# First weights, convolution steps, prompt set-up and sample loads moved to earlier stages of a two-layer hybrid decoder step

## The chip, the core and the metric

The kernel runs on one core of a Trainium2 chip. A core has TensorE (PE, matrix products into PSUM), VectorE (DVE), ScalarE (ACT), GpSimd (POOL) and SyncE (SP, which mainly issues DMA transfers); each follows a program of its own, and they wait for one another with semaphores. The metric is the device time of one execution in microseconds (us).

## The reference

One inference step of a decoder trunk of two layers, for a prompt of 1024 rows and for 8 samples that each add one row to a past of 4096. Cut to what the change touches:

```python
h = _rmsnorm(x, norm_pre_mix[l])
z = h @ w_in[l]                                    # 1024 -> all columns of four head groups
gconv, gdn_conv = _causal_dwconv(st['gdn_conv'], gqkv, gdn_conv_w[l])      # width 4, 768 columns
gq, gk, gv = jnp.split(jax.nn.silu(gconv), 3, axis=-1)                     # gq, gk then L2-normalised
y = concat(retention(..), mlstm(..), gated_delta(..), nsa(..))             # 4 heads of 64 each
x = x + _rmsnorm(y @ w_out[l], norm_post_mix[l])
x = x + _rmsnorm(conv_ffn(_rmsnorm(x, norm_pre_ffn[l])), norm_post_ffn[l])
```

mLSTM and the gated delta rule need gates: log-sigmoids and softplus of eight columns of z each (mi, mf, ga, gbeta), their running sums along the rows and a running maximum. nsa attends to compressed, selected and windowed keys; for the samples these come from paged caches.

## The kernel before

**Stages.** `first_stage` normalises the input and builds tables. Then each layer runs `project_in` (z), `recurrent_prompt`, `recurrent_sample`, `nsa_prompt`, `nsa_sample` and `dense` (output projection and FFN). Between two stages all engines meet (`kit.clear`, `kit.next_stage`): nothing of the next stage starts before the last DMA that the present one awaits has landed.

**project_in (L427)** goes over 8 chunks of columns (`CHUNKS`, 468 wide, the last 464) and in each over 9 tiles of 128 rows; the ninth holds the samples. Tile number n is 9 times the chunk plus t, from 0 to 71. Every value is split into a high and a low part, so a prompt tile is 8 k-slices of three matmuls (L565, L569, L570), a sample tile 8 of two (L565, L567). A tile's sum is copied out of one of 8 PSUM banks by ACT (t = 0, 2, 4, 6; L608) or DVE (t = 1, 3, 5, 7, and 8, the samples', with L656 and L657), and SP stores it to z (L538) from one of 8 buffers. Beside that, tiles 0 to 7 of a chunk split the next chunk's weights, a k-slice per tile: ACT makes the high part (`high`, L600), DVE the low part (`low`, L646), the latter as the last thing of the tile's slot in DVE's program. PE awaits the k-th low part (`lo_ready`) at the first tile of a chunk.

**The convolution** of the prompt rides along in 8 steps j of 128 rows, at tile numbers fixed by three tables: `conv_in` (SP, four shifted copies of z into one buffer, L518, after the silu of step j-1), then POOL without a table (four products L580, two sums L581, L582, later a root L584), `conv_act` (DVE sum L665, ACT tanh L614, DVE silu L667, and square, sum and eps L668 to L672), `conv_scale` (DVE L678, L679) and SP's store to g_conv (L522).

**recurrent_prompt** begins with a set-up: SP loads bias vectors, eight gate columns of z twice, tables (`r_upper` to `r_gains`) and the first tiles' heads; DVE, ACT and PE turn the gates into sums, maxima and decays for all 8 tiles (DVE L1950 to L1998, PE L1616 to L1627); two rows of results go through DRAM and back as a broadcast (`r_rows`, `r_brow`). Then comes the loop over the tiles, whose first use of it is L2138 to L2198. SP issues the samples' loads (`beside`, tiles `d_...`) behind the set-up, and the third tile's heads after those.

**nsa_prompt** stores its rows of y_mix as they are done (y_stored) and awaits the stores. **nsa_sample** starts with the loads of its queries (zq), position terms (per, pev_in), compression weights (wk, `e_kT`) and window cache (win); DVE clears buffers (L3457 to L3462, L3466) around the first scaling L3464; PE's first product is L3202; POOL loads cache pages (L3054).

Of the kernel before, what the change touches and what calls it, by code (L numbers as in the profile page):

```python
# [112 lines left out]
def program(nc, io):  # L113
    with ExitStack() as ctx:
# [23 lines left out]
        heads_ahead = ctx.enter_context(nc.semaphore("heads_ahead"))  # L138
        first_copies = ctx.enter_context(nc.semaphore("first_copies"))
# [5 lines left out]
        first_stage(kit, env, io, tabs)  # L145
        kit.next_stage()

        for l in range(DEPTH):
            with ExitStack() as c:
                h_hi = sb(c, "h_hi", [P, KD, ROWS], F32R)  # L150
                h_lo = sb(c, "h_lo", [P, KD, ROWS], F32R)
                project_in(kit, env, io, l, h_hi, h_lo)
            kit.next_stage()
            if io.get("mixers", True):
                mixers(kit, env, io, l)
            with ExitStack() as c:
                ahead = sb(c, "w_ahead", [P, 4, D])
                nsa_sample(kit, env, io, l, ahead)
# [126 lines left out]
def first_stage(kit, env, io, tabs):  # L285
# [5 lines left out]
    with ExitStack() as c:  # L291
# [10 lines left out]
        low3 = sb("t_low3", [P, 1], I32)  # L302

        with nc.Block() as b:
            @b.sync
            def _(sp):
# [36 lines left out]
                st.all_in()  # L343

# [29 lines left out]
            def _(act):  # L374
# [8 lines left out]
                act.wait_ge(S("row_stored"), 16)  # L383
                norm_stored(kit, act)
                for h in range(H):
                    act.dma_start(env["wdist"][h], env["wrow"][h].partition_broadcast(P)).then_inc(env["first_copies"], 16)
                act.dma_start(x_cur[0:SEQ, :], io["x_prompt"][0]).then_inc(env["first_copies"], 16)

            @b.vector
            def _(dve):  # L390
# [13 lines left out]
                for t in range(TT):  # L404
# [22 lines left out]
def project_in(kit, env, io, l, h_hi, h_lo):  # L427
# [6 lines left out]
    CHUNKS = (4, 5, 6, 0, 1, 2, 3, 7)  # L434
# [15 lines left out]
    A_TILES, V_TILES = (0, 2, 4, 6), (1, 3, 5, 7, SAMPLE)  # L450

# [8 lines left out]
    with ExitStack() as c:  # L460
# [5 lines left out]
        raw = sb("zi_raw", [P, 3 * PART, ZC])  # L466
        w_hi = sb("zi_whi", [P, 2, KD, ZC], F32R)
        w_lo = sb("zi_wlo", [P, 2, KD, ZC], F32R)
# [4 lines left out]
        low_z = sb("zi_low", [NB, ZC])  # L473
        zs = h[:].rearrange("p a k n -> p (a k n)").rearrange("p (j n) -> p j n", n=768)
# [7 lines left out]
        with nc.Block(no_gpsimd_drain=True) as b:  # L482
            @b.sync
            def _(sp):
# [5 lines left out]
                def load(i, half):  # L490
                    u = 2 * i + half
                    if u >= 3:
                        sp.wait_ge(S("lo_ready"), PART * (u - 2))
# [5 lines left out]
                for k in range(0, KD, 2):  # L499
                    a = CHUNKS[0] * ZC  # L500
                    sp.dma_start(raw[:, k:k + 2], io["w_in"][ds(l, 1), k * P:k * P + 2 * P, a:a + ZC]
                                 .rearrange("a (k p) n -> p (a k) n", p=P)).then_inc(S(f"w_first{k // 2}"), 16)
# [21 lines left out]
                for i in range(NZ):  # L524
                    for t in range(TT):
# [26 lines left out]
            def _(pe):  # L552
                for i in range(NZ):
                    for t in range(TT):
# [3 lines left out]
                        if n >= NBK:  # L558
                            z_wait(pe, n - NBK)
                        for k in range(KD):  # L560
                            if t == 0:
                                pe.wait_ge(S("lo_ready"), KD * i + k + 1)
                            rows_hi, rows_lo = h_hi[:, k, cols(t)], h_lo[:, k, cols(t)]
                            out, c0 = ps[:, n % NBK, 0:span(i)], slice(0, span(i))
                            nc.tensor.matmul(out, rows_hi, w_hi[:, i % 2, k, c0], start=(k == 0), stop=False)  # L565
                            if t == SAMPLE:
                                m = nc.tensor.matmul(out, rows_hi, w_lo[:, i % 2, k, c0], start=False, stop=(k == KD - 1))  # L567
                                continue
                            nc.tensor.matmul(out, rows_hi, w_lo[:, i % 2, k, c0], start=False, stop=False)  # L569
                            m = nc.tensor.matmul(out, rows_lo, w_hi[:, i % 2, k, c0], start=False, stop=(k == KD - 1))  # L570
                        m.then_inc(S("z_summed"), 1)

# [14 lines left out]
            def _(act):  # L587
                def h_high(t):
# [3 lines left out]
                def high(i, k):  # L592
# [7 lines left out]
                    A.activation(w_hi[:, i % 2, k, 0:span(i)], raw[:, part(i, k), 0:span(i)], ACT.Copy).then_inc(S("hi_ready"), 1)  # L600

                def chunk(i, t):
                    n = i * TT + t
                    if t in A_TILES:
# [3 lines left out]
                        A.activation(zo[:, n % NZO, 0:span(i)], ps[:, n % NBK, 0:span(i)], ACT.Copy).then_inc(S("z_by_act"), 1)  # L608
                    if n in conv_act:
# [4 lines left out]
                        A.activation(conved(j), zs[:, 0], ACT.Tanh, scale=0.5).then_inc(S("x_tanh"), 1)  # L614
                    if t < KD and i + 1 < NZ:
# [3 lines left out]
                for k in range(KD):  # L619
# [3002 lines left out]
```

## Time and profile before

| | us |
|---|---|
| median of 3 runs | 4123.53 |
| lowest and highest | 4115.71 and 4125.43 |
| the profiled execution | 4113.04 |
| its span | 4111.3 |
| PE busy | 3677.8 (89%) |
| DVE, ACT, POOL busy | 1908.6, 1260.1, 411.4 |

The span runs from the first to the last record of the profiled execution. PE's granted clock has two levels, 1.2 and 2.4 GHz; the profile gives it as a share of the higher, on average 0.946.

### The profile page before, as it was taken

To read this page: it belongs to the slowest core of one execution; us is meant where nothing else is said; L and a number is where in the kernel's file an instruction comes from. 1 tells how busy PE (TensorE), PEld (TensorE's weight loads), DVE (VectorE), ACT (ScalarE), POOL (GpSimd) and SP (SyncE) were. 2 spreads that over 40 slices of the span, in tenths; PEclk is the share of its full clock that TensorE was granted. 3 is DMA by queue.
4 is the path that set the end of the run, shared out by engine and by line. 5 is a ranking of instruction groups with operands and counts; after the bars stand their busy time and mean duration, and the time that the engine had idled before them with its cause. 6 is when DMAs were issued, how large, how long until landed. Compare 5 with 4: busy or idle time off the path is not lost. (4 is left out here: it accounts for less than half of the span.)

```text
span 4111.3 us, 55178 instructions
## 1 busy us (share of the span) xinstructions
PE 3677.8 (89%) x22004; PEld 3151.8 (77%) x22004; DVE 1908.6 (46%) x3752; ACT 1260.1 (31%) x2863; POOL 411.4 (10%) x287
## 2 busy tenths in 40 slices
PE   5999697698979999999979996967798999999998
PEld 3888587446668999997768885854465799999875
DVE  3234487663444333335541336875533543333345
ACT  2111265452222212124331113645422321121333
POOL 0035101002100000000000550010021100000000
PEclk9999799798989999999989997978898999999999
DMA  7344332306332222255542433332252422222653
GB/s 241 130 145 148 100 110 83 103 7 221 161 123 90 65 75 64 76 189 192 199 156 92 165 129 110 99 96 58 90 213 94 152 64 78 62 78 62 231 180 134
DMA packets 304475, 499.98 MB, mean 122 GB/s; under 512 B 66757, under 2 KB 228325, under 8 KB 299632
## 3 DMA queue, kind: packets, MB, share of 16 engines
q1 hardware_dynamic: 298955, 421.21, 32.1%
q0 software_dynamic: 4608, 67.11, 4.0%
q10 hardware_dynamic: 656, 8.13, 0.6%
q8 instruction: 175, 2.87, 0.3%
q14 instruction: 81, 0.66, 0.1%
HBM read 395.16 MB, written 116.52 MB: 124 GB/s over the span
## 5 line engine op out<-in xcount | busy, mean ns | idle before, releaser
L1042 PE MATMUL ps<-h_hi,fu_hi 128*128 128x344 f32 x2112 | 682.3, 323 | 10.1 <-DVE h_lo L1266 7.3
L1044 PE MATMUL ps<-h_hi,fu_lo 128*128 128x344 f32 x2112 | 677.5, 321 | 0.0
L1043 PE MATMUL ps<-h_lo,fu_hi 128*128 128x344 f32 x2112 | 677.1, 321 | 0.0
L565 PE MATMUL ps<-zi_whi,h_hi 128*128 128x468 f32 (+1 forms) x1152 | 433.4, 376 | 49.6 <-DVE zi_wlo L646 49.6
L1042 PEld LDWEIGHTS ps<-h_hi,fu_hi 128*128 128x128 f32 x2112 | 398.1, 188 | 14.1 <-DVE h_lo L1266 7.8
L1044 PEld LDWEIGHTS ps<-h_hi,fu_lo 128*128 128x128 f32 x2112 | 398.8, 189 | 0.0
L1043 PEld LDWEIGHTS ps<-h_lo,fu_hi 128*128 128x128 f32 x2112 | 398.2, 189 | 0.0
L569 PE MATMUL ps<-zi_wlo,h_hi 128*128 128x468 f32 (+1 forms) x1024 | 384.5, 375 | 0.0
L570 PE MATMUL ps<-zi_whi,h_lo 128*128 128x468 f32 (+1 forms) x1024 | 384.1, 375 | 0.0
L1068 PE MATMUL ps<-fd_whi,fd_fhi 128*128 128x512 f32 x704 | 276.6, 393 | 15.0 <-DVE fd_flo L1283 14.2
L565 PEld LDWEIGHTS ps<-zi_whi,h_hi 128*128 128x128 f32 x1152 | 217.6, 189 | 79.2 <-DVE h_lo L642 50.8
L1070 PE MATMUL ps<-fd_whi,fd_flo 128*128 128x512 f32 x704 | 275.3, 391 | 0.0
L1069 PE MATMUL ps<-fd_wlo,fd_fhi 128*128 128x512 f32 x704 | 274.6, 390 | 0.0
L570 PEld LDWEIGHTS ps<-zi_whi,h_lo 128*128 128x128 f32 x1024 | 193.4, 189 | 25.4
L569 PEld LDWEIGHTS ps<-zi_wlo,h_hi 128*128 128x128 f32 x1024 | 193.6, 189 | 24.7
L1277 DVE TENSOR_TENSOR fd_wlo<-w_ahead,fd_whi 128x1024 fp32r<-128x1024 f32 x88 | 107.7, 1224 | 176.8 <-ACT fd_whi L1131 176.8
L1356 DVE TENSOR_TENSOR fu_f<-fu_c,ps 128x344 f32<-128x344 f32 x132 | 67.2, 512 | 239.6 <-PE ps L1044 187.2
L608 ACT ACTIVATE zi_z<-ps 128x468 f32<-128x468 f32 (+1 forms) x64 | 35.7, 559 | 450.6 <-PE ps L570 450.6
L646 DVE TENSOR_TENSOR zi_wlo<-zi_raw,zi_whi 128x468 fp32r<-128x468 f32 (+1 forms) x128 | 96.9, 764 | 165.0 <-ACT zi_whi L600 163.9
L1344 DVE TENSOR_SCALAR fu_c<-fu_g,fu_side 128x1024 f32<-128x1024 f32 x44 | 33.1, 753 | 301.2 <-ACT fu_g L1176 301.1
L1068 PEld LDWEIGHTS ps<-fd_whi,fd_fhi 128*128 128x128 f32 x704 | 132.6, 188 | 51.0 <-DVE fd_wlo L1277 18.6
L580 POOL TENSOR_TENSOR zi_h<-zi_h,zi_cw 128x768 f32<-128x768 f32 x64 | 123.0, 1922 | 464.6 <-DMA zi_h<-z 460.9
(624 smaller groups left out, 6736.4 us busy)
## 6 DMA issues: line engine op xcount, KB each, us to landing
w_ahead<-w_ffn_down SPq DMA_DIRECT2D x44, 1024.0 KB, 5.5
z<-zi_z SPq DMA_DIRECT2D x112, 234.0 KB
zi_h<-z SPq DMA_DIRECT2D x64, 384.0 KB, 4.6
f_all<-fu_f SPq DMA_DIRECT2D x44, 516.0 KB, 3.3
w_ahead<-w_ffn_gate SPq DMA_DIRECT2D x44, 512.0 KB, 4.8
w_ahead<-w_ffn_up SPq DMA_DIRECT2D x44, 512.0 KB, 6.1
fd_raw<-w_ffn_down SPq DMA_DIRECT2D x22, 1024.0 KB, 5.7
zi_raw<-w_in SPq DMA_DIRECT2D x24, 936.0 KB, 5.5
```

Of the source, the lines that this page charges most:

```text
L565: nc.tensor.matmul(out, rows_hi, w_hi[:, i % 2, k, c0], start=(k == 0), stop=False)
L569: nc.tensor.matmul(out, rows_hi, w_lo[:, i % 2, k, c0], start=False, stop=False)
L570: m = nc.tensor.matmul(out, rows_lo, w_hi[:, i % 2, k, c0], start=False, stop=(k == KD - 1))
L580: link(G_.tensor_tensor(zs[:, k], zs[:, k], cw[:, k, :], ALU.mult))
L646: V.tensor_tensor(w_lo[:, i % 2, k, 0:span(i)], raw[:, part(i, k), 0:span(i)], w_hi[:, i % 2, k, 0:span(i)].bitcast(F32), ALU.subtract).th ...
L1042: nc.tensor.matmul(out, up_hi[f % 2][:, j, k, :], h_hi[:, k, seg], start=(k == 0), stop=False)
L1043: nc.tensor.matmul(out, up_hi[f % 2][:, j, k, :], h_lo[:, k, seg], start=False, stop=False)
L1044: m = nc.tensor.matmul(out, up_lo[f % 2][:, j, k, :], h_hi[:, k, seg], start=False, stop=(k == KD - 1))
L1068: nc.tensor.matmul(out, hi, w_hi[:, q, part], start=(f == 0), stop=False)
L1069: nc.tensor.matmul(out, hi, w_lo[:, q, part], start=False, stop=False)
L1070: m = nc.tensor.matmul(out, lo, w_hi[:, q, part], start=False, stop=(f == NF - 1))
L1277: V.tensor_tensor(w_lo[:, q], raw(pp)[:, f % 2], w_hi[:, q].bitcast(F32), ALU.subtract).then_inc(S("w_low"), 1)
```

## The change

- **First stage.** The four loads of layer 0's first weights (`first_weights`) are issued by SP after the third row store, and ACT and DVE make their eight high and low parts at the stage's end. For layer 0, `SPLIT` = 8 slices then need no splitting in project_in. The copies of `wdist` (four) and `x_cur` leave ACT's queue; SP issues them in layer 0's project_in at tile 11 (`first_copies`).
- **project_in, both layers.** Convolution steps stand 4 tiles apart in place of 5. The last chunk (`FINAL`, tiles 63 to 71) uses six PSUM banks; the other two serve the set-up of recurrent_prompt (`PromptSetup`), which moves into that chunk: SP loads at tile 62, DVE, ACT and PE pieces between tiles 64 and 70, rows out and back at 68, 69, 70 and at the end. Tiles that live across the border have fixed places (`PromptEarly`).
- **recurrent_prompt** starts without the set-up.
- **nsa_prompt** issues the samples' first loads (`SampleEarly.load`) before its y stores; its last two y stores count on `rows_ahead`, which nsa_sample awaits (POOL before page load 1, ACT before `wT`, SP at its end).
- **nsa_sample** starts with these loads done; all of DVE's clearing but one stands behind the copies that PE's next products read.

```diff
+def first_weights(sp, io, l, E, k, sem):
+    a = CHUNKS[0] * ZC
+    sp.dma_start(E.raw[:, k:k + 2], io["w_in"][ds(l, 1), k * P:k * P + 2 * P, a:a + ZC]
+                 .rearrange("a (k p) n -> p (a k) n", p=P)).then_inc(sem, 16)
+def first_copies(sp, env, io):
+    for h in range(H):
+        sp.dma_start(env["wdist"][h], env["wrow"][h].partition_broadcast(P)).then_inc(env["first_copies"], 16)
+    sp.dma_start(env["x_cur"][0:SEQ, :], io["x_prompt"][0]).then_inc(env["first_copies"], 16)
...
+                    if t == 2:
+                        for k in range(0, KD, 2):
+                            first_weights(sp, io, 0, E, k, S(f"w_first{k // 2}"))
...
-                act.wait_ge(S("row_stored"), 16)
-                norm_stored(kit, act)
-                for h in range(H):
-                    act.dma_start(env["wdist"][h], env["wrow"][h].partition_broadcast(P)).then_inc(env["first_copies"], 16)
-                act.dma_start(x_cur[0:SEQ, :], io["x_prompt"][0]).then_inc(env["first_copies"], 16)
+                for k in range(KD):
+                    if k % 2 == 0:
+                        act.wait_ge(S(f"w_first{k // 2}"), 16)
+                    nc.scalar.activation(E.w_hi[:, k], E.raw[:, k], ACT.Copy).then_inc(S("first_high"), 1)
...
+                for k in range(KD):
+                    dve.wait_ge(S("first_high"), k + 1)
+                    V.tensor_tensor(E.w_lo[:, k], E.raw[:, k], E.w_hi[:, k].bitcast(F32), ALU.subtract)
...
-    conv_in = {29 + 5 * j: j for j in range(NT)}
-    conv_act = {33 + 5 * j: j for j in range(NT)}
-    conv_scale = {34 + 5 * j: j for j in range(NT)}
+    SPLIT = KD if l == 0 else 0
+    conv_in = {29 + 4 * j: j for j in range(NT)}
+    conv_act = {32 + 4 * j: j for j in range(NT)}
+    conv_scale = {33 + 4 * j: j for j in range(NT)}
+    FINAL = (NZ - 1) * TT
...
+        return n % NBK if n < FINAL else (n - FINAL) % 6
...
+                        if l == 0 and n == TT + 2:
+                            first_copies(sp, env, io)
...
+                        if n == FINAL - 1:
+                            sp.wait_ge(S("lo_ready"), KD * NZ - SPLIT)
+                            setup.tables(sp)
+                            for k in range(NZO):
+                                sp.wait_ge(S(f"z_stored{k}"), 16 * len(range(k, FINAL, NZO)))
+                            setup.gate_columns(sp)
+                            sp.wait_ge(S("x_stored0"), 16)
+                            sp.wait_ge(S("z_summed"), FINAL)
+                            setup.first_heads(sp)
+                        if n == FINAL + 5:
+                            setup.rows_out(sp, 0)
+                        if n == FINAL + 6:
+                            setup.rows_back(sp, 0)
+                        if n == FINAL + 7:
+                            setup.rows_out(sp, 1)
+                setup.rows_back(sp, 1)
+                setup.all_in(sp)
...
+                        if n == FINAL + 2:
+                            z_wait(pe, users[6][-1])
+                            setup.pe_sums(pe)
...
+                    if n == FINAL + 1:
+                        setup.dve_gates(dve, link)
+                    if n == FINAL + 2:
+                        setup.dve_decays(dve, link)
+                    if n == FINAL + 3:
+                        setup.dve_scan(dve, link)
+                    if n == FINAL + 4:
+                        setup.dve_max(dve, link)
+                        setup.dve_shifts(dve, link)
+                    if n == FINAL + 7:
+                        setup.dve_rows(dve, link)
...
+                F.load(env, io, l, sp)
...
-                    sp.dma_start(y_mix[t * P:t * P + P, 768:1024], y[:, k % 2].rearrange("p h d -> p (h d)")).then_inc(S(f"y_stored{k % 2}"), 16)
+                    sp.dma_start(y_mix[t * P:t * P + P, 768:1024], y[:, k % 2].rearrange("p h d -> p (h d)")).then_inc(
+                        S(f"y_stored{k % 2}") if k < NT - 2 else env["rows_ahead"], 16)
...
-                pool.wait_ge(S("ld"), 16 * 4)
+                pool.wait_ge(env["start_ahead"], 16 * 4)
                 load(0)
-                pool.wait_ge(S("win_in"), 16)
+                pool.wait_ge(env["win_ahead"], 16)
+                pool.wait_ge(env["rows_ahead"], 32)
```

**DVE in chunk 6 of project_in, before the change.** `zi_wlo` (464 wide) is a weight split for the last chunk, `zi_z<-ps` an eviction, `zi_low` and the row after it that of the sample tile, `zi_h<-zi_h` begins a convolution step's `conv_act` and `zi_xc<-zi_xc,zi_ss` ends its `conv_scale`. These are the rows from the end of step 5 to step 7.

```order
L679 TENSOR_TENSOR zi_xc<-zi_xc,zi_ss_465 128x512
L646 TENSOR_TENSOR zi_wlo<-zi_raw,zi_whi 128x464 x2
L659 COPY zi_z<-ps 128x468
L646 TENSOR_TENSOR zi_wlo<-zi_raw,zi_whi 128x464
L656 COPY zi_low<-ps 8x468
L657 TENSOR_TENSOR zi_z<-ps,zi_low 8x468
L665 TENSOR_TENSOR zi_h<-zi_h 128x768
L667 SCALAR_TENSOR_TENSOR zi_xc<-zi_xc,zi_h 128x768
L668 TENSOR_TENSOR zi_sq<-zi_xc 128x512
L671 TENSOR_REDUCE zi_ss_465<-zi_sq 128x8
L672 TENSOR_SCALAR zi_ss_465<-zi_ss_465 128x8
L659 COPY zi_z<-ps 128x464
```

The same place with the change, the end of chunk 6 (tiles 60 to 63):

```order
L720 TENSOR_TENSOR zi_wlo_535<-zi_raw_58,zi_whi_534 128x464
L739 TENSOR_TENSOR zi_h<-zi_h 128x768
L741 SCALAR_TENSOR_TENSOR zi_xc<-zi_xc,zi_h 128x768
L742 TENSOR_TENSOR zi_sq<-zi_xc 128x512
L745 TENSOR_REDUCE zi_ss_539<-zi_sq 128x8
L746 TENSOR_SCALAR zi_ss_539<-zi_ss_539 128x8
L720 TENSOR_TENSOR zi_wlo_535<-zi_raw_58,zi_whi_534 128x464
L733 COPY zi_z<-ps 128x468
L752 TENSOR_TENSOR zi_ss_539<-zi_ss_539,zi_qks 128x8
L753 TENSOR_TENSOR zi_xc<-zi_xc,zi_ss_539 128x512
L720 TENSOR_TENSOR zi_wlo_535<-zi_raw_58,zi_whi_534 128x464
L730 COPY zi_low<-ps 8x468
```

Before, the last two splits stand ahead of step 6 and two steps follow in the last chunk; now step 7 itself stands ahead of the last two splits.

**SP around the border of the last chunk, before:** `z<-zi_z` are the z stores (8x464 is tile 71, the last), `r_...` the set-up's loads in the next stage.

```order
L538 DMA z<-zi_z 8x464
L522 DMA g_conv<-zi_xc 128x768
L482 UNCONDITIONAL_BRANCH
L2252 UNCONDITIONAL_BRANCH
L80 DMA r_gates<-mlstm_b_i 128x4
L80 DMA r_gates<-mlstm_b_f 128x4
L80 DMA r_gates<-gdn_dt_bias 128x4
L80 DMA r_gates<-gdn_A_log 128x4
L80 DMA r_zsm<-z 128x8x8 x2
L80 DMA r_upper<-c_upper 128x128
L80 DMA r_xq<-g_conv 128x512
L80 DMA r_zq<-z 128x512 x2
```

And with the change, from the gate columns' load behind the store of tile 62 (the tables' thirteen loads stand ahead of these rows) to the end of the stage:

```order
L80 DMA r_zsm_71<-z 128x8x8 x2
L80 DMA r_xq_82<-g_conv 128x512
L80 DMA r_zq_81<-z 128x512 x2
L574 DMA z<-zi_z 128x464
L556 DMA g_conv<-zi_xc 128x768
L574 DMA z<-zi_z 128x464 x5
L1634 DMA r_rows<-r_rows_79 32x128
L574 DMA z<-zi_z 128x464
L1641 DMA r_brow_80<-r_rows 128x512 x2
L574 DMA z<-zi_z 128x464
L1634 DMA r_rows<-r_rows_79 32x128
L574 DMA z<-zi_z 8x464
```

The loads moved past the stage's border and past nine z stores; the rows' round trip is woven into the last stores.

## Rows read from the trace of the kernel before

**Rows 1.** Busy time on the page: us, share of the span, instructions.

```profile
PE 3677.8 (89%) x22004; PEld 3151.8 (77%) x22004; DVE 1908.6 (46%) x3752; ACT 1260.1 (31%) x2863; POOL 411.4 (10%) x287
```

**Rows 2.** Windows: us, busy PE, PEld, DVE, ACT, POOL, granted clock, DMA share, GB/s.

```profile
100.00:400.00 300.00, 300.00 (x1416) 265.51 (x1416) 97.13 (x143) 52.07 (x94) 83.75 (x44) 1.00 0.43 144
...
953.00:966.00 13.00, 11.97 (x87) 11.78 (x85) 3.94 (x14) 2.86 (x7) 4.73 (x3) 0.50 1.00 426
```

**Rows 3.** Timeline (start, us, engine) and a DMA landing: both layers' projection starts.

```profile
55.88 0.41 DVE L423 COPY t_cmp<-ps 4x256 f32<-4x256 f32 x1
...
55.10 4.70 SPq L80 DMA_DIRECT2D z<-zrow  x4
...
56.10 4.42 ACTq L386 DMA_DIRECT2D wdist<-wrow  x4
...
68.93 0.34 SPq L488 DMA_DIRECT2D zi_h<-h_next  x1
...
92.05 0.73 PE L565 MATMUL ps<-zi_whi,h_hi 128*128 128x468 f32 x1 [36.99 <-DVE zi_wlo L646]
...
h_next<-st_n_h SPq DMA_DIRECT2D x2, 512.0 KB, 2.6
...
2101.51 0.32 SPq L488 DMA_DIRECT2D zi_h<-h_next  x1
...
2106.25 1.23 DVE L642 TENSOR_TENSOR h_lo<-zi_h,h_hi 128x1024 fp32r<-128x1024 f32 x1 [9.27 <-ACT h_hi L590]
```

**Rows 4.** Timeline of the convolution: POOL, then SP, then DVE.

```profile
249.71 1.86 POOL L580 TENSOR_TENSOR zi_h<-zi_h,zi_cw 128x768 f32<-128x768 f32 x1 [202.99 <-DMA zi_h<-z]
...
349.69 7.94 POOL L580 TENSOR_TENSOR zi_h<-zi_h,zi_cw 128x768 f32<-128x768 f32 x4 [3.49 <-DMA zi_h<-z]
...
359.91 1.84 POOL L582 TENSOR_TENSOR zi_h<-zi_h 128x768 f32<-128x768 f32 x1
...
372.12 3.81 POOL L580 TENSOR_TENSOR zi_h<-zi_h,zi_cw 128x768 f32<-128x768 f32 x2 [4.01 <-DMA zi_h<-z]
...
365.12 1.88 SPq L518 DMA_DIRECT2D zi_h<-z  x4
...
363.73 0.96 DVE L667 SCALAR_TENSOR_TENSOR zi_xc<-zi_xc,zi_h 128x768 f32<-128x768 f32 x1 [0.98 <-ACT zi_xc L614]
...
368.45 0.69 DVE L679 TENSOR_TENSOR zi_xc<-zi_xc,zi_ss 128x512 f32<-128x512 f32 x1
369.18 0.64 DVE L646 TENSOR_TENSOR zi_wlo<-zi_raw,zi_whi 128x464 fp32r<-128x464 f32 x1
```

**Rows 5.** Timeline: evictions of tile 63 (ACT) and tile 71 (DVE).

```profile
408.28 0.56 ACT L608 ACTIVATE zi_z<-ps 128x464 f32<-128x464 f32 x1 [12.05 <-PE ps L570]
...
447.22 0.63 DVE L656 COPY zi_low<-ps 8x464 f32<-8x464 f32 x1 [2.70 <-PE ps L567]
```

**Rows 6.** Timeline of the head of recurrent_prompt, layer 0: SP, DVE, PE.

```profile
452.35 0.34 SPq L80 DMA_DIRECT2D r_gates<-mlstm_b_i  x1
...
462.56 0.43 SPq L80 DMA_DIRECT2D r_gains<-gdn_norm  x1
...
478.29 1.76 SPq L1507 DMA_DIRECT2D r_brow<-r_rows  x4
...
513.47 0.33 SPq L80 DMA_DIRECT2D r_xq<-g_conv  x1
...
458.05 0.19 DVE L1950 TENSOR_TENSOR r_qa<-r_zsm,r_gates 128x32 f32<-128x32 f32 x1 [4.81 <-DMA r_upper<-c_upper]
...
486.49 0.69 DVE L2198 TENSOR_TENSOR r_NLT<-ps,r_w 128x512 f32<-128x512 f32 x1 [0.98 <-ACT r_w L1895]
...
461.98 0.69 PE L1616 MATMUL ps<-r_qa,r_upper 128*128 128x64 f32 x2 [14.87 <-DVE r_qa L1961]
```

**Rows 7.** Timeline: last row of nsa_prompt (DVE), first product of nsa_sample (PE), layer 0.

```profile
929.74 0.43 DVE L2849 TENSOR_TENSOR p_y<-p_y,p_ysw 128x256 f32<-128x256 f32 x1
...
941.88 0.56 PE L3202 MATMUL ps<-ident,e_kT 8*128 8x8 f32 x4 [13.44 <-DVE e_kT L3464]
```

More of the change, by code:

```diff
@@ L142, in program @@
         env = dict(locals())
-        first_stage(kit, env, io, tabs)
+        early = [PromptEarly(nc, l) for l in range(DEPTH)]
+        first_stage(kit, env, io, tabs, early[0])
         kit.next_stage()
         for l in range(DEPTH):
+            E = early[l]
             with ExitStack() as c:
@@ L302, in first_stage @@
         low3 = sb("t_low3", [P, 1], I32)
+        assert nc.sbuf_base <= E.start
         with nc.Block() as b:
@@ L424, in first_stage, with project_in @@
         kit.clear()
-def project_in(kit, env, io, l, h_hi, h_lo):
+def project_in(kit, env, io, l, h_hi, h_lo, E):
     nc, S, ps, z, mhalf = kit.nc, kit.sem, env["ps"], env["z"], env["mhalf"]
@@ L450, in project_in, with bank @@
     A_TILES, V_TILES = (0, 2, 4, 6), (1, 3, 5, 7, SAMPLE)
+    def bank(n):
+        return n % NBK if n < FINAL else (n - FINAL) % 6
+    users = [[n for n in range(NZ * TT) if bank(n) == k] for k in range(NBK)]
     def z_wait(eng, n):
@@ L473, in project_in @@
         low_z = sb("zi_low", [NB, ZC])
+        assert nc.sbuf_base <= E.start
+        setup = PromptSetup(kit, env, io, l, E)
         zs = h[:].rearrange("p a k n -> p (a k n)").rearrange("p (j n) -> p j n", n=768)
@@ L498, in _ @@
                 load_h(0)
[L499 to L502, printed above, removed]
+                for k in range(SPLIT, KD, 2):
+                    first_weights(sp, io, l, E, k, S(f"w_first{k // 2}"))
                 load_h(1)
@@ L599, in high @@
                         act.wait_ge(S("z_summed"), TT * (i - 1))
-                    A.activation(w_hi[:, i % 2, k, 0:span(i)], raw[:, part(i, k), 0:span(i)], ACT.Copy).then_inc(S("hi_ready"), 1)
+                    A.activation(w_hi[i % 2][:, k, 0:span(i)], raw[:, part(i, k), 0:span(i)], ACT.Copy).then_inc(S("hi_ready"), 1)
                 def chunk(i, t):
@@ L618, in _ @@
                 h_high(0)
-                for k in range(KD):
+                for k in range(SPLIT, KD):
                     high(0, k)
@@ L683, in _ @@
                 h_rest(0)
-                for k in range(KD):
+                for k in range(SPLIT, KD):
                     low(0, k)
@@ L1450, in __init__, with sb @@
         self.fq, self.fk = sb("fq", NT, H), sb("fk", NT, H)
-        def nc_t(name, shape, dt):
-            return nc.sbuf_tensor(name, shape, dt, allow_name_mangling=True)
-        self.scan = ctx.enter_context(nc_t("r_scan", [32, 2, 64 + P], F32))
-        self.rows = ctx.enter_context(nc_t("r_rows", [32, 2, P], F32))
-        self.brow = sb("brow", 2, 2, H, P)
+        self.scan = at("r_scan", [32, 2, 64 + P])
+        self.rows = at("r_rows", [32, 2, P])
+        assert at.at <= self.start + RAW_BYTES
+        at = Place(nc, self.start + RAW_BYTES, l)
+        self.brow, self.zq, self.xq = at("r_brow", [P, 2, 2, H, P]), at("r_zq", [P, 2, 4, 256]), at("r_xq", [P, 2, 8, HD])
+        assert at.at <= TOP
+class PromptTiles:
+    def __init__(self, nc, ctx, states, E):
+        def sb(name, *shape):
+            return ctx.enter_context(nc.sbuf_tensor("r_" + name, [P, *shape], F32, allow_name_mangling=True))
+        self.upper, self.maskT, self.last, self.ones, self.lev, self.lev0T, self.xi = E.upper, E.maskT, E.last, E.ones, E.lev, E.lev0T, E.xi
+        self.rope, self.gains, self.gates, self.zsm, self.qa, self.ends, self.mp, self.ml = E.rope, E.gains, E.gates, E.zsm, E.qa, E.ends, E.mp, E.ml
+        self.fq, self.fk, self.scan, self.rows, self.brow, self.zq, self.xq = E.fq, E.fk, E.scan, E.rows, E.brow, E.zq, E.xq
+        self.Sret, self.Caug, self.Sgdn, self.mprev = states.Sret, states.Caug, states.Sgdn, states.mprev
+        self.vr, self.vm, self.gz = sb("vr", 2, 256), sb("vm", 2, H, HD + 1), sb("gz", 2, 3, 256)
         self.ta, self.tb, self.qk = sb("ta", 8, HD), sb("tb", 8, HD), sb("qk", 2, 8, HD)
@@ L1524, in values_in @@
             ld(R.gz[:, q, j, :], z[r0:r0 + P, a:a + 256])
-    ld = Loads(sp, S("gates_in"))
-    for j, name in enumerate(("mlstm_b_i", "mlstm_b_f", "gdn_dt_bias", "gdn_A_log")):
-        ld(R.gates[:, 4 * j:4 * j + 4], vector(name))
-    ld(R.zsm[:, 0], tiles(MI, 8))
-    ld(R.zsm[:, 1], tiles(GA, 8))
-    ld(R.upper[:], io["c_upper"])
-    heads_in(0)
-    ldc = Loads(sp, S("tables_in"))
-    ldc(R.rope[:], io["c_rope"][0:SEQ].rearrange("(t p) n -> p t n", p=P))
-    ldc(R.xi[:].rearrange("p a h -> p (a h)"), io["c_xi"])
-    ldc(R.last[:], io["c_last"])
-    ldc(R.maskT[:], io["c_maskT"])
-    ldc(R.lev[:].rearrange("p a n -> p (a n)"), io["c_lev"][:, 0:(STEPS + 1) * P])
-    ldc(R.lev0T[:], io["c_levT"][:, 0:P])
-    for j, name in enumerate(("ret_norm", "mlstm_norm", "gdn_norm")):
-        ldc(R.gains[:, j, :], vector(name))
     values_in(0)
@@ L1544, in prompt_sync @@
     values_in(1)
-    for k, ready in enumerate(("decay_rows", "max_rows")):
-        sp.wait_ge(S(ready), 1)
-        sp.dma_start(env["r_rows"][k].rearrange("t (h n) -> (t h) n", h=H), R.rows[:, k]).then_inc(S("rows_stored"), 16)
-    sp.wait_ge(S("rows_stored"), 32)
-    rows_in(0)
-    rows_in(1)
     beside(Loads(sp, env["kept"]))
@@ L2717, in nsa_prompt @@
         scl = sb("p_scl", [P, H, 3])
+        assert nc.sbuf_base <= F.start + (NHALF - 2) * 16384
         with nc.Block(no_gpsimd_drain=True) as b:
@@ L2989, in nsa_sample @@
         AHEAD = 2
+        assert nc.sbuf_base <= F.start
         def slot(i):
```

415 lines of the change are left out of this document (262 added, 153 removed).

## The prediction

> **What bounds the kernel now.** I read the busy shares first: TensorE (PE) works 89% of the span [rows 1], so an edit pays only where PE stands still. The windows show that the projection stage is not such a place: between 100 and 400 us PE is busy for 300.00 of 300.00 us at a granted clock of 1.00, while VectorE (DVE) works 97, ScalarE (ACT) 52 and GpSimd (POOL) 84 us [rows 2]. Then I went through the timeline at the stages' edges, where PE is idle: 36.99 us before layer 0's first projection matmul [rows 3], 14.87 us at the head of the prompt's recurrence [rows 6] and 13.44 us at the head of the sample's attention [rows 7]; the last two come once a layer. The change touches these three, about 94 us together. To make room it also packs the convolution tighter, and that part lies in the stage that has no slack, so I looked at its chain last [rows 4].
>
> **The measure.** A change below 0.3% (12 us of 4123.5) cannot be told from none. The profiled execution took 4113.04 us, its span 4111.3 and 1.7 around it; the median of the three runs is 4123.53, 10.5 higher. I sum differences on the profile's rows and put the sum on the median.
>
> **1. Start of layer 0: -21 us.** Project_in begins at 68.93 and its first matmul at 92.05 [rows 3]. Before it, DVE ends at 55.88 + 0.41 = 56.3; SP has issued its last zero stores at 55.10 + 4.70 = 59.8; ACT's four copies of wdist (960 KB each) and one of x_prompt follow from 56.10 [rows 3]. The change adds eight subtractions to DVE; at 0.64 us, the duration of such a one [rows 4], DVE ends near 61.4. The copies are gone from here, so the zero stores should land like an h_next store, 2.6 us after issue [rows 3], at 62.4. With 2 us for the barrier the stage starts at about 64.5; ends 62.5 (barrier free) and 68.93 (nothing gained). From there layer 1 gives the pace when no copies are in the way: h load issued 2101.51, h_lo done at 2106.25 + 1.23 = 2107.5 [rows 3], 6.0 us, and with the first weights split already PE can start then: 70.6 against 92.05, **-21.4** (-17 to -23.5). Layer 1's start keeps its shape: 0.
>
> The copies now stand on SP's queue in front of the z store of tile 11. Issued at ACT's price of 4.42 for four and, for the fifth, no more than as much again, they hold SP for under 9 us, in which two tiles' stores are late; eight output buffers cover it, since a tile is 24 matmuls of 300.00 / 1416 = 0.212 us [rows 2], 5.08. A weight load behind them needs to be in only when the next chunk begins. Cost 0; without the cover, 9.
>
> **2. Convolution every 4 tiles: +30 us a layer at the last chunk's start.** A step is a closed chain, because the loads of step j+1 wait until DVE has made the silu of step j. Follow one: SP issues its loads at 365.12, POOL begins at 372.12, 7.0 us later; POOL's six operations of the step before ran from 349.69 to 359.91 + 1.84 = 361.75, 12.06 us; DVE's and ACT's part ends with the silu at 363.73 + 0.96 = 364.69, 2.94; SP then issues after 0.43. Together 22.4, and the two starts 349.69 and 372.12 are 22.43 apart [rows 4]. At five tiles a step (5 x 5.08 = 25.4) the loop keeps up; at four (20.3) it cannot. It becomes the bound, because in DVE's program of chunk 6 the last two weight splits now stand behind convolution steps 6 and 7, as the first pair of excerpts shows, and PE's tile 63 needs them.
>
> The loop is longer than 22.4 where its load slot belongs to a tile that DVE evicts: SP then waits for an eviction that stands behind square, sum, eps, a split and the eviction itself on DVE: some 0.69 + 0.69 + 0.17 + 0.64 + 0.64 = 2.8 (0.69 and 0.64 as in [rows 4]; the short one 0.17). That holds for four of the seven periods (load slots 37, 41, 53, 57). So 3 x 22.4 + 4 x 25.2 = 168. POOL's step 0 is placed as before and ends near 261.8 (249.71 + 12.06 [rows 4]). Step 7 leaves POOL at 429.8; its scaled output is 7.4 later (from 361.75 to 368.45 + 0.69 = 369.14 [rows 4]), 437.2; then the last split 0.64. PE ends tile 63 a little after, 438.6 by my count, where its eviction now starts at 408.28 [rows 5]: **+30**. If the load slots cost nothing, 7 x 22.4 = 157 and it is +19; if every slot costs 2.8 and PE restarts slowly, +34. PE also stops at chunk 6's start, since the last of its splits now stands behind step 5's silu; that is not added, because the loop and not PE sets the end of step 7.
>
> **3. The setup in the last chunk: +10 more.** SP may load the tables only after the last split and the z store of tile 62: from 439.4. The recurrence's first nineteen issues take 452.35 to 462.99, 10.64 us [rows 6]; the sixteen of them up to the gate columns, 16/19, are 8.9, and 2.6 for landing [rows 3]: 450.9. The gate chain on DVE and ACT takes 461.98 - 458.05 = 3.9 to PE's first product [rows 6], and about 0.8 of memsets come ahead of it: 455.6. PE has ended tile 65 at 438.6 + 10.1 = 448.7, so it waits 7 us. Then 5 tiles of 5.08, the short tile (3.4) and 2 us of small products: the last eviction at 486.4 against 447.22 [rows 5], +39.2. The stage ends 5.1 us behind it now (452.35 [rows 6]); with the second row broadcast behind the last store (half of the 1.76 of issue [rows 6], 2.6 of landing, the barrier) I take 6.3. PE's six banks in place of eight there, the tiles' fixed addresses and two more semaphore clears on POOL cost 0: evictions follow within one tile, and without that cover a tile, 5.08. Together **+40.4 a layer** (29 to 46: the lower end where the load slots are free, the upper where PE restarts at the lower clock after each of its new waits).
>
> **4. Head of the recurrence: -21 us a layer.** Now the first score product of tile 0 is masked by DVE at 486.49, 34.1 us after 452.35 [rows 6]. Without the setup what is left of that is the rope and the masks: 8.2 or less, since 486.49 - 478.29 = 8.2 still has the wait for the broadcast in it, and I leave that in for the stage's start: -26. But SP's loads for the samples, from 480.05 until 513.47, are 33.4 us of issue [rows 6], and now start at the stage's beginning. Heads of tile 2 come behind them: now 27.0 us after 486.49, then 7.2 (fifteen issues of values and heads at 0.48, a gains issue with its gap) + 33.4 - 8.2 = 32.4 after. Of these 5.4 us I take 5 as a new wait, which no row prices (0 to 5.4). **-21** (-26 to -20).
>
> **5. Head of the sample's attention: -10 us a layer.** The prompt's last rows are ready at 930.17; PE's first product comes 11.7 us later at 941.88, released by DVE's first work on the loaded tile [rows 7]. With these loads made in the stage before, and the last two stores (2.6 landing [rows 3]) no longer awaited, the stage starts near 931.0 and PE's product stands 0.7 behind it: 10.2 earlier. DVE's memsets move behind what PE waits for; I count nothing for them. POOL, ACT and SP await the two stores later, 2.6 us after their issue, and none of them has work that early but POOL's page loads 1 and on, which queue behind load 0 anyway. The five loads stand on SP's queue ahead of the y stores, which wait for y. **-10.2** (-8 to -12).
>
> **Sum.** Per layer 40.4 - 21 - 10.2 = +9.2; two layers +18.4; with the start -21.4: **-3 us**. So no change that can be measured: 4120.5. Term by term the ends are 2 x (29 - 26 - 12) - 23.5 = -41 and 2 x (46 - 20 - 8) - 17 = +19.
>
> **Where a rule and a row differ.** Between 953 and 966 PE is busy 11.97 of 13.00 us and its granted clock is still 0.50, the lower level [rows 2]. The Trainium skill (TensorE: Matmul & The Clock Gate, Part 1) says that the lower clock is the default and that sustained matmul work releases it; by that, work so dense should run at the upper level, and does not in this row. By the row an earlier start alone buys no clock, and I count none.
>
> **The rivals.**
> *A. The clock stays up in the sample's attention.* PE's idle time before it shrinks from 13.44 to a few us; if the level then holds through the first 13 dense us, half of 11.97, 6.0 us a layer, is gained on top, 12 in all: 4108. Against it: little work precedes that stretch. By the page's rule above this is the natural outcome. Chance 0.13.
> *B. The convolution's lag is hidden.* If the loop ran at the four-tile pace, POOL would be done in time, terms 2 and 3 would shrink to the few products on PE (+2 a layer), and the sum is 2 x (2 - 21 - 10.2) - 21.4 = -80: 4044. Against it: 22.43 between two starts [rows 4] where nothing but the chain held it. Chance 0.07.
> *C. The tail costs more: slower.* Mechanism: the setup chain passes five times between DVE, PE and ACT in the last chunk, in front of evictions and in the middle of PE's tiles; each passage that misses its slot stops PE, which now flows in that chunk without a gap. Price: the same passages took 478.29 - 461.98 = 16.3 us at the recurrence's head [rows 6], 2.6 of it a store's landing; if these 13.7 are exposed here in full and nothing of term 4 is lost, 2 x 13.7 - 3 = +24: 4148. It decides when the gate columns land after tile 66 would end (453.8). Chance 0.2.
> *D. The change does not do what it says at the start:* the first stage still ends at 68.93, or the h loads still take 20 us because SP's issue, not the copies, is slow. Then only -2 of the -21 is left, sum +16: 4140. Against it: layer 1. Chance 0.05.
> *My forecast* keeps 0.55, of which 0.12 lies under -12 us and 0.06 over +12.
>
> **How the numbers follow.** Faster by over 0.3%: 0.12 + 0.07 + 0.10 of A = 0.29, and I raise it to 0.33 because the lower end of my own terms is the longer one. Slower: 0.06 + 0.20 + 0.05 = 0.31, less 0.04 for cases of C that stay under 12 us: 0.27. The same: 0.40. The range leaves B out and most of C's upper half: from 4123.5 - 41 = 4082.5 to 4148. The likeliest case alone spans 4082 to 4143.
>
> **What would show it.** Right: first projection matmul near 70 us; POOL's steps starting 22 to 26 us apart; PE idle for some 15 us at chunk 6's start and 10 or more at chunk 7's, released by the weight splits; a wait of about 7 us on the gate sums; no PE wait at the heads of recurrence and sample attention; project_in 40 us longer in layer 1. Wrong: steps 20 us apart without PE idle in the stage (B), or a stage that is longer by 55 (C).

## The result, and the profile after

The changed kernel takes 4138.93 us (median of 6 runs, 4130.30 to 4145.18), the kernel before, in its runs beside it, 4121.98 (6 runs). The ratio is 1.0038, 95% interval 1.0021 to 1.0055: **slower by 0.4%**, 15.7 us, where -3 us and no measurable change had been forecast. The profiled execution has a span of 4127.2 us against 4111.3, +15.9, so its rows stand for the difference.

The stages' lengths, read from the first instruction behind each barrier in the two traces (us, after minus before):

| | forecast | layer 0 | layer 1 |
|---|---|---|---|
| to the first projection matmul of layer 0 | -21.4 | -19.0 | |
| projection stage | +40.4 a layer | +43.2 | +41.8 |
| prompt's recurrence | -21 a layer | -16.4 | -14.4 |
| samples' recurrence to the end of the samples' attention | -10.2 a layer | -4.9 | -17.5 |
| dense | 0 | +0.7 | +2.5 |

The sum is +16.0. In the fourth row the two layers differ because nsa_prompt itself takes 170 to 177 us from one pass to the next in both kernels, at granted clocks between 0.87 and 0.91 over the stage; it was the longer one in layer 0 after the change and in layer 1 before. Their mean, -11.2, is the number to compare. nsa_sample by itself went from 224.3 to 214.2 us in layer 0 and from 227.1 to 214.4 in layer 1, 10.1 and 12.7 less.

**The page and a window over the projection stage.** The first row answers to [rows 1]. The second fence is the window view of the whole stage of layer 0, from its first matmul to the next stage, of the changed kernel (columns as in [rows 2]).

```profile
PE 3697.1 (90%) x22004; PEld 3162.4 (77%) x22004; DVE 1900.3 (46%) x3752; ACT 1259.1 (31%) x2863; POOL 406.5 (10%) x287
```

```profile
73.03:476.48 403.45, 367.34 (x1674) 321.31 (x1674) 120.99 (x233) 61.97 (x110) 104.89 (x56) 0.95 0.46 151
```

The same window of the kernel before:

```profile
92.05:452.34 360.29, 355.06 (x1664) 313.99 (x1664) 120.33 (x175) 62.25 (x109) 107.45 (x56) 1.00 0.41 139
```

PE now stands still for 36.1 of 403.45 us where it stood for 5.2 of 360.29, and it is busy for 12.3 us longer, with ten products of the set-up in the window and a granted clock of 0.95 in place of 1.00. "90% busy" on the page hides both.

**Start of layer 0** (timeline of the changed kernel, answers to [rows 3]): the eight subtractions, the first h load, the first matmul.

```profile
57.83 4.53 DVE L439 TENSOR_TENSOR zi_wlo<-zi_raw,zi_whi 128x468 fp32r<-128x468 f32 x8
...
67.01 6.31 SPq L524 DMA_DIRECT2D zi_h<-h_next  x4
...
73.03 0.76 PE L619 MATMUL ps<-zi_whi,h_hi 128*128 128x468 f32 x1 [13.44 <-DVE h_lo L716]
```

The first matmul stands 6.0 us behind the h load, as forecast; the stage itself began at 67.0, not 64.5. Other kernels below with the same first stage began it between 64.45 and 66.85, so most of these 2.5 us vary from one execution to the next.

**The convolution and the last chunk** (timeline, POOL, PE, ACT, DVE; answers to [rows 4, 5]):

```profile
372.43 7.90 POOL L646 TENSOR_TENSOR zi_h<-zi_h,zi_cw 128x768 f32<-128x768 f32 x4 [7.53 <-DMA zi_h<-z]
...
398.09 7.63 POOL L646 TENSOR_TENSOR zi_h<-zi_h,zi_cw 128x768 f32<-128x768 f32 x4 [7.16 <-DMA zi_h<-z]
...
407.74 1.84 POOL L648 TENSOR_TENSOR zi_h<-zi_h 128x768 f32<-128x768 f32 x1
```

```profile
345.40 0.58 PE L619 MATMUL ps<-zi_whi,h_hi 128*128 128x468 f32 x1 [2.27 <-DVE zi_wlo L720]
363.46 0.76 PE L619 MATMUL ps<-zi_whi,h_hi 128*128 128x468 f32 x1 [14.27 <-DVE zi_wlo L720]
...
414.88 0.75 PE L619 MATMUL ps<-zi_whi,h_hi 128*128 128x464 f32 x1 [4.97 <-DVE zi_wlo L720]
418.06 0.75 PE L619 MATMUL ps<-zi_whi,h_hi 128*128 128x464 f32 x1 [1.65 <-DVE zi_wlo L720]
...
436.45 0.66 PE L1654 MATMUL ps<-r_qa,r_upper 128*128 128x64 f32 x2 [4.64 <-DVE r_qa L1727]
```

```profile
419.68 0.56 ACT L676 ACTIVATE zi_z<-ps 128x464 f32<-128x464 f32 x1 [7.28 <-PE ps L624]
...
468.95 0.63 DVE L730 COPY zi_low<-ps 8x464 f32<-8x464 f32 x1 [2.67 <-PE ps L621]
```

POOL's steps are 21.5 to 25.7 us apart, and from the start of step 0 to that of step 7 it is 167.8 us (398.09 - 230.28), where 168 was forecast. Step 7 leaves POOL at 407.74 + 1.84 = 409.58; put back by the 19.0 us of the earlier start this is 428.6, where 429.8 was forecast. PE waits for weight splits at both chunks' starts (2.27 + 14.27 and 4.97 + 1.65). Tile 63 is evicted at 419.68, 438.7 on the old clock (forecast 438.6), and tile 71 at 468.95, 488.0 (486.4).

**Head of the recurrence** (timeline of SP, DVE and PE, answers to [rows 6]): the first value load, the first masked score, the third tile's heads as issued and as awaited.

```profile
478.56 0.32 SPq L80 DMA_DIRECT2D r_vr<-z  x1
...
519.31 0.33 SPq L80 DMA_DIRECT2D r_xq<-g_conv  x1
...
484.73 0.69 DVE L2400 TENSOR_TENSOR r_NLT<-ps,r_w 128x512 f32<-128x512 f32 x1 [1.38 <-PE ps L1993]
...
526.19 1.11 PE L1881 MATMUL ps<-ident,r_xq 128*128 128x128 f32 x4 [7.41 <-DMA r_zq<-z]
```

The masked score comes 8.2 us behind the stage's start at 476.48 (forecast 8.2). But SP issues the third tile's heads 34.6 us behind that score, after 85 loads for the samples, and PE stands for 7.41 us until they land; in layer 1 it stands for 6.90. Behind the wait the granted clock is lower for a few microseconds (a window of the changed kernel, columns as in [rows 2]):

```profile
526.00:532.00 6.00, 5.81 (x39) 5.40 (x40) 2.51 (x5) 3.13 (x8) 0.00 (x0) 0.67 1.03 314
```

**Head of the samples' attention** (timeline, answers to [rows 7]): PE's wait there is down from 13.44 to 4.39. The second fence is the window over the stage's first 16 us.

```profile
947.07 0.56 PE L3425 MATMUL ps<-ident,e_kT 8*128 8x8 f32 x4 [4.39 <-DVE e_kT L3682]
```

```profile
946.00:962.00 16.00, 11.71 (x90) 11.31 (x90) 11.18 (x23) 6.77 (x12) 7.20 (x7) 0.57 0.80 324
```

### The profile page after: what moved, and what is told of

Same layout as the page of the kernel before. It is cut to its first block and busy times, and to the rows that moved or that the text cites. A ratio compares the mean times of both kernels' runs of the same rounds, so it can differ in the third digit from the quotient of the medians.

```text
span 4127.2 us, 55193 instructions
## 1 busy us (share of the span) xinstructions
PE 3697.1 (90%) x22004; PEld 3162.4 (77%) x22004; DVE 1900.3 (46%) x3752; ACT 1259.1 (31%) x2863; POOL 406.5 (10%) x287
## 5 line engine op out<-in xcount | busy, mean ns | idle before, releaser
L619 PE MATMUL ps<-zi_whi,h_hi 128*128 128x468 f32 (+1 forms) x1152 | 442.3, 384 | 73.9 <-DVE zi_wlo L720 60.0
L1127 PEld LDWEIGHTS ps<-h_hi,fu_hi 128*128 128x128 f32 x2112 | 398.1, 188 | 15.5 <-DVE h_lo L1351 7.8
L1261 ACT ACTIVATE fu_g<-ps 128x344 f32<-128x344 f32 x132 | 60.3, 458 | 349.3 <-PE ps L1129 349.2
L1216 ACT ACTIVATE fd_whi<-w_ahead 128x1024 fp32r<-128x1024 f32 x88 | 93.2, 1059 | 219.2 <-PE ps L1155 151.2
```

What stands on the lines that cost most here:

```text
L619: nc.tensor.matmul(out, rows_hi, w_hi[i % 2][:, k, c0], start=(k == 0), stop=False)
L1127: nc.tensor.matmul(out, up_hi[f % 2][:, j, k, :], h_hi[:, k, seg], start=(k == 0), stop=False)
L1216: A.activation(w_hi[:, q], raw(pp)[:, f % 2], ACT.Copy).then_inc(S("w_high"), 1)
```

## The experiments

Theory after the result: the convolution's loop holds the weight splits and costs 30 us a layer, the third tile's heads behind the samples' loads cost 7 to 9, and the other parts bring what was forecast. Main rival: the setup in the last chunk is what costs (rival C).

### Steps at five tiles again

The first experiment puts only the three tables back.

```diff
-    conv_in = {29 + 4 * j: j for j in range(NT)}
-    conv_act = {32 + 4 * j: j for j in range(NT)}
-    conv_scale = {33 + 4 * j: j for j in range(NT)}
+    conv_in = {29 + 5 * j: j for j in range(NT)}
+    conv_act = {33 + 5 * j: j for j in range(NT)}
+    conv_scale = {34 + 5 * j: j for j in range(NT)}
```

> The changed kernel with the convolution steps back at five tiles (loads at tile 29+5j, sum and silu at 33+5j, scale at 34+5j), everything else as changed. Theory (the convolution's loop, 22 to 26 us a step, holds the last weight splits and through them tile 63): the 30 us a layer are gone and only the setup's own cost of some 6 to 9 us stays in the last chunk; project_in of layer 0 from its first matmul to the next stage takes about 368 us, where the change has 403 and the kernel before 360; the whole about 68 us below the changed kernel, some 4070. Rival (the setup in the last chunk is what costs): the stage stays within 10 us of 403 and the whole within 20 us of 4139.

Measured: 4078.91 us (4 runs), ratio to the kernel before 0.9899 (0.9882 to 0.9915). The changed kernel stood at 1.0038, so these three lines are worth 1.4%, 57 us. The window over layer 0's projection stage:

```profile
70.65:447.29 376.64, 361.80 (x1674) 319.49 (x1674) 131.09 (x233) 62.40 (x110) 107.45 (x57) 0.98 0.49 162
```

PE's wait for weight splits is gone there, and the stage is 26.8 us shorter than the changed kernel's 403.45. It is not the 368 expected: with the setup in the last chunk it still costs 16.4 us more than before, not 6 to 9. By this window 9.6 of them are idle time of PE and 6.7 busy time, at a granted clock of 0.98. In layer 1 the stage is 15.5 us longer than before. Some of the idle time is looked at below; the rest is not traced to a row. The rival falls as the cause of the slowdown, though the setup costs more than either side gave it.

### Steps at four tiles, and nothing else

> The kernel before with the convolution steps four tiles apart and nothing else of the change. Theory: PE stands still at the starts of chunks 6 and 7 (about 15 and 14 us or more in all, 30 a layer), project_in is 30 us longer in both layers and the whole about 4122 + 60 = 4182. Rival (the setup costs): PE idles for nothing in project_in and the time is that of the kernel before, 4122, or a few us less.

The edit is the same three lines the other way, in the kernel before. Measured: 4186.83 us (4 runs), ratio 1.0150 (1.0133 to 1.0167), +62 us where +60 was expected. PE's waits in its timeline, chunk 6 and chunk 7 of layer 0:

```profile
381.96 0.76 PE L565 MATMUL ps<-zi_whi,h_hi 128*128 128x468 f32 x1 [14.62 <-DVE zi_wlo L646]
...
432.64 0.76 PE L565 MATMUL ps<-zi_whi,h_hi 128*128 128x464 f32 x1 [5.24 <-DVE zi_wlo L646]
435.81 0.76 PE L565 MATMUL ps<-zi_whi,h_hi 128*128 128x464 f32 x1 [1.64 <-DVE zi_wlo L646]
```

They are those of the changed kernel within 0.4 us, without any setup in the chunk. Layer 0's stage, 92.34 to 481.79, is 29.2 us longer than before. In layer 1 it is 30.7 us longer. That settles the second term from both sides. It also gives the setup's share in the changed kernel: 43.2 - 29.2 = 14.0 us in layer 0 and 41.8 - 30.7 = 11.1 in layer 1.

### The third tile's heads before the samples' loads

```diff
     values_in(1)
-    beside(Loads(sp, env["kept"]))
     for t in range(NT + 1):
         if t + 2 < NT:
             heads_in(t + 2)
             rows_in(t + 2)
+        if t == 0:
+            beside(Loads(sp, env["kept"]))
```

> The changed kernel, with the third tile's heads and rows issued before the samples' 70 or so small loads instead of behind them. Theory (SP's 33 us of issue make PE and DVE wait for the heads of tile 2): PE's wait of 7.4 us on that load goes, in both layers, and with it the slower clock after it; 7 to 9 us a layer, the whole about 4123. Rival (the wait only shows up there and the loop is held by something else, such as the values' loads): another wait of 5 to 7 us takes its place within the first three tiles, and the whole stays at 4139 within 4 us.

Measured: 4119.53 us (10 runs), ratio 0.9994 (0.9980 to 1.0008); against 1.0038 that is some 18 us, 9 a layer. SP issues the heads at 485.35, and PE takes them without a wait (timelines of SP and PE):

```profile
485.35 0.32 SPq L80 DMA_DIRECT2D r_xq<-g_conv  x1
...
515.85 0.60 PE L1882 MATMUL ps<-ident,r_xq 128*128 128x128 f32 x4
```

The masked score of tile 0 came at 481.99, so PE reaches tile 2 33.9 us later, where the changed kernel needed 526.19 - 484.73 = 41.5 and the kernel before some 34.6. No other wait took the place. The stage takes 248.7 and 246.6 us in the two layers, 9.2 and 13.5 less than in the changed kernel. That is more than the waits of 7.41 and 6.90 because the products behind them ran slower: the four that take 0.60 us here took 1.11 there.

### Both edits

> Both edits: steps at five tiles, and the third tile's heads before the samples' loads. Theory: the gains add up, about 68 + 16 below the changed kernel, 4055, which is also below the kernel before by some 65. Rival for the head (another wait takes its place): 4070, as with the first edit alone. Rival for the steps (setup costs): near 4123.

Measured: 4065.33 us (4 runs), ratio 0.9858 (0.9837 to 0.9878), 58 us **below the kernel before**. 4055 had been expected; the 10 missing are the setup's own cost, which the first experiment had shown already. The stages tell what moving the setup is worth here: the recurrence is 25.5 and 25.1 us shorter than in the kernel before, the projection from its first matmul on 13.3 and 16.5 us longer, so that 12 and 9 us a layer are left.

### The two other parts alone

The start alone: the kernel before with `first_weights`, `first_copies`, the splits in the first stage and `SPLIT`, nothing else of the change.

> The kernel before with the first stage's part alone: layer 0's first weights loaded and split there, the wdist and x_prompt copies on SP at tile 11; steps at five tiles, no other move. Theory: layer 0's first projection matmul at 70 to 73 us in place of 92, no new wait behind the copies, the whole 19 to 21 us below the kernel before, 4102. Rival (the copies cost later what they free at the start, as late stores or weight loads on SP's queue): a wait of PE in chunks 1 or 2 and a gain under 12.

Measured: 4103.85 us (6 runs), ratio 0.9946 (0.9925 to 0.9967), some 22 us. The first matmul stands at 71.00, and PE waits for no store or weight in chunks 1 and 2, although SP issues the copies at tile 11 (129.21 to 132.40 us, 3.2 in all).

The samples' attention alone: the kernel before with `SampleEarly`, `rows_ahead` and DVE's clearing moved.

> The kernel before with the sample attention's part alone: its first loads issued in the prompt's attention, the last two row stores awaited later, DVE's clearing moved. Theory: PE's wait of 13.4 us at the head falls to 4 to 5, both layers together 18 to 24 us less, the whole about 4102. Rival (the page loads bound that stretch, so an earlier start only moves the wait to the staged pages): under 10 us in all.

Measured: 4105.20 us (5 runs), ratio 0.9937 (0.9917 to 0.9958), some 26 us, 13 a layer; PE's wait at the head is 4.38 and 4.37 us. Each part does what the forecast's first and fifth terms gave it, or a little more.

### What the setup still costs

In the kernel with both edits PE waits 5.8 and 3.4 us for the gate sums. This kernel loads what the gates need first:

```diff
-        self.ldc = ldc = Loads(sp, self.kit.sem("tables_in"))
-        ldc(R.upper[:], io["c_upper"])
+        self.ldf = ldf = Loads(sp, self.kit.sem("gate_tables_in"))
...
+        ldf(R.upper[:], io["c_upper"])
+    def later_tables(self, sp):
...
                             setup.gate_columns(sp)
+                            setup.later_tables(sp)
```

The gates await `gate_tables_in`; `pe_ends` and `dve_max` await `tables_in`.

> Steps at five tiles and the third tile's heads first, as before, and the setup's loads in another order: the four bias vectors and the triangle first, with a semaphore of their own, then the gate columns, then the other eight tables, which only the maximum and the shifts await. Theory (the setup chain in the last chunk starts with the landing of 13 tables and the columns): PE's wait on the gate sums, 5.8 and 3.4 us in the two layers, goes, 3 to 5 us a layer, the whole 6 to 10 below 4065. Rival (the chain waits for DVE's convolution step 6 instead, whose scale stands ahead of the gates): the wait stays and so does the time, within 4 us.

Measured: 4062.05 us (5 runs), ratio 0.9840 (0.9821 to 0.9860), the lowest of the study, but not told apart from 0.9858. PE's wait is still 4.0 and 3.4 us: the rival holds. DVE's timeline shows what is ahead of the gates (the end of step 6's scale, then the setup's first operation), and something that had not been looked for, the seven operations of the running maximum:

```profile
395.64 0.69 DVE L754 TENSOR_TENSOR zi_xc<-zi_xc,zi_ss 128x512 f32<-128x512 f32 x1
396.42 0.17 DVE L1724 MEMSET r_ones<- 128x128 f32 x1
...
410.70 7.20 DVE L1761 TENSOR_TENSOR r_scan<-r_scan 32x128 f32<-32x128 f32 x7
```

In the kernel before, where POOL does nothing at that time, the same seven took 2.16 us, and in the changed kernel, where the convolution is over by then, too:

```profile
445.68 2.16 DVE L1750 TENSOR_TENSOR r_scan<-r_scan 32x128 f32<-32x128 f32 x7
```

Here POOL works on step 7 beside them (405.42 to 416.8). The last kernel moves every step one tile earlier (28, 32, 33 + 5j), so that step 6's scale no longer stands ahead of the gates.

> The last kernel (steps at five tiles, third heads first, gate tables first) with every convolution step one tile earlier: loads at 28+5j, sum and silu at 32+5j, scale at 33+5j, so step 6 is scaled at tile 63 and no longer at 64 ahead of the gates. Theory (step 6's scale on DVE holds the gates, DVE reached them at 396.4 us while the columns had landed some 5 us before): PE's wait on the gate sums, 4.0 and 3.4 us, falls under 1; 3 us a layer, the whole some 6 below 4062. Rival (POOL's step 7 now runs beside the gates, as it ran beside the scan, whose seven small operations took 7.20 us there and 2.16 in the kernel before): the wait stays at 3 us or more, the scan gets back to some 2 to 3 us, and the time is within 4 us of 4062.

Measured: 4066.48 us (4 runs), ratio 0.9862 (0.9842 to 0.9883): no gain. Both expectations are half right. The wait on the gate sums falls to 0.58 and 0.84 us, as the theory says. The rival had the right neighbour and the wrong operations: the gates are free of POOL's step 7, but the maximum now lies beside it but for its last operation, takes 11.29 us, and PE waits 7.37 for it (timelines of POOL, DVE and PE):

```profile
405.19 7.53 POOL L647 TENSOR_TENSOR zi_h<-zi_h,zi_cw 128x768 f32<-128x768 f32 x4 [13.97 <-DMA zi_h<-z]
...
412.79 1.80 POOL L648 TENSOR_TENSOR zi_h<-zi_h 128x768 f32<-128x768 f32 x1
414.67 1.80 POOL L649 TENSOR_TENSOR zi_h<-zi_h 128x768 f32<-128x768 f32 x1
...
405.64 11.29 DVE L1761 TENSOR_TENSOR r_scan<-r_scan 32x128 f32<-32x128 f32 x7
...
416.98 0.31 PE L1678 MATMUL ps<-ident,r_scan 32*128 32x32 f32 x1 [7.37 <-DVE r_scan L1761]
```

The wait has moved and not shrunk. For gate sums and maximum together PE stood 7.4 us in layer 0 and 8.1 in layer 1 in the kernel before this one, and stands 8.0 and 8.3 here.

A placement in which the maximum misses both POOL's step and DVE's was not tried; it is open what it would bring.

## Why the prediction was wrong

It forecast no measurable change, from terms of opposite sign of some 81 and 84 us that nearly cancelled; what it got wrong is 19 us in their sizes, which the cancelling left standing. Only one term, by the mean of the two layers, lies outside the range that was given for it: the head of the recurrence.

- **Start, -21.4:** right in mechanism, 19.0 in the trace of the whole change; alone 21.1 in the trace (92.05 - 71.00) and 22 measured. The copies cost nothing at their new place.
- **Convolution every 4 tiles, +30 a layer:** right, to 0.1 us at tile 63 and with +62 for both layers measured alone. The mechanism (loads wait for the silu, splits stand behind the steps on DVE) is shown by the first two experiments, which undo and isolate it. Only PE's wait at chunk 7 was smaller than the 10 us named, 6.6, since much of the lag already falls on chunk 6.
- **Setup in the last chunk, +10 more:** between the evictions of tiles 63 and 71 the stage got 10.3 us longer, forecast 9.2 to the last eviction, and PE's wait on the gate sums was 4.64 and not 7. Right in mechanism and a little small: the stage as a whole is 43.2 and 41.8 longer, where 40.4 was forecast, and the upper end given, 46, holds it. Beside steps at five tiles the setup costs 16.4 and 15.5, which this term, at 10.4, would have missed.
- **Head of the recurrence, -21 a layer: the step that failed.** The first part, -26, is right: 8.2 us to the first masked score, and with the third tile's heads first the whole stage is 25.6 and 27.9 us shorter than before. The sentence "Of these 5.4 us I take 5 as a new wait, which no row prices (0 to 5.4)" is not: PE waits 7.41 and 6.90, and the third experiment gives 9 a layer back. Two things were left out. The first value load waits for POOL's clearing of the tiles it fills and stands 2.1 us behind the stage's start (478.56 against 476.48), as does all of SP's queue behind it. With it the shift in issue is 34.6 against 27.0 us behind the masked score, 7.6, where the bound was drawn at 5.4, as if the issue began with the stage. And a wait of 7 us on PE costs the slower clock after it, here four products in 1.11 us for 0.60, at a granted clock of 0.67 between 526 and 532 us (1.00 from the same products on, 515.85 to 521.85, in the third experiment). The third experiment prices the two together at 9.2 and 13.5 us of the stage (9.6 in both layers between the kernels with steps at five tiles), where 5 was taken. The stage gained 16.4 and 14.4, so 11 of the 19 us are here. The forecast was also not at one with itself: it counted 5 us of wait in the sum and named "no PE wait at the heads of recurrence" as a sign of being right.
- **Head of the samples' attention, -10.2 a layer:** -11.2 in the mean of the two layers, 26 us for both alone. Right, a little small.
- **Rivals.** C named the right sign for the wrong place: its 13.7 us a layer in the last chunk did not come on top of the sum, only 3.6 and 0.7 did (14.0 and 11.1 for 10.4). A (the clock stays up) did not happen: between 946 and 962 us, the stage's first 16, the granted clock was 0.57. PE was busy for 11.71 of those 16 us, so this is no second case of work as dense as in the row of the kernel before, and nothing more is shown of the rule that was set beside it. B fell with the first pair of experiments, D with the start.
- **The remaining miss** is small terms: 2.4 at the start and 3 in dense, where nothing was changed, which one execution of each kernel does not tell from chance, and 4 in the two projection stages; some 2 came back at the samples' attention.

In one respect the forecast had everything in hand and did not say it: it priced the four-tile steps at +60 and everything else at about -63. By its own numbers, the parts without the steps would have been the better kernel, as the experiments then showed with -58 us.

## What to carry to other kernels

A change in parts is worth summing part by part, and then asking of each part with a cost whether the others need it: three lines held 57 us back here. Before a step is packed tighter, follow its loop once around all engines and queues and compare it with the new pace; 22.4 us a step in a slot of 20.3 made the loop the bound, and what is queued behind its waits in program order (here the last weight splits) carried it to PE. And when a stage's head is emptied, look at what its DMA queue does next: many small loads that nobody needs yet were harmless behind a set-up and stood in the way without it.

## What the runs showed of the hardware

A DVE operation with two inputs from SBUF waited for POOL here. In the last kernel each of the first six maxima of 32x128 ends within 0.2 us after one POOL operation of 1.8 us on its 128x768 tile has ended, and takes 1.5 to 1.9 us. The seventh, in the same sequence, begins when POOL's step is over and takes 0.28, as each of the seven does in the kernel before (timelines of POOL and DVE, the sixth and seventh):

```profile
414.67 1.80 POOL L649 TENSOR_TENSOR zi_h<-zi_h 128x768 f32<-128x768 f32 x1
...
414.76 1.84 DVE L1761 TENSOR_TENSOR r_scan<-r_scan 32x128 f32<-32x128 f32 x1
...
416.64 0.28 DVE L1761 TENSOR_TENSOR r_scan<-r_scan 32x128 f32<-32x128 f32 x1
```

The kernel before has it too, in its weight splits (timelines of POOL and DVE):

```profile
257.73 1.84 POOL L581 TENSOR_TENSOR zi_h<-zi_h 128x768 f32<-128x768 f32 x1
...
257.83 2.23 DVE L646 TENSOR_TENSOR zi_wlo<-zi_raw,zi_whi 128x468 fp32r<-128x468 f32 x1
```

The 23 splits of its two projection stages that begin while POOL computes on that tile take 0.63 to 2.32 us, and each ends 0.50 to 0.63 us after the POOL operation; the others take 0.63 to 0.65, and so do the copies from PSUM, with POOL busy or not. The Trainium skill (GPSIMD Engine Reference, Specifications) says that GpSimd shares its SBUF interfaces with VectorE and that DVE instructions with two SBUF inputs contend; the trace agrees. The forecast's one price from rows for the setup on DVE was read where POOL was idle.

The copies that took ACT 4.42 us to issue at the first stage's end took SP 2.54 at tile 11: the cost of issuing the same transfers was not the same at the two places.
